# First modulation weights in four pairs, two token-feature tiles normed and projected per pair

## What is computed

```
mod   = silu(c)     @ w_mod[0] + b_mod[0]      # 6 x 1024 values for latent tokens
mod_c = silu(c_ctx) @ w_mod[0] + b_mod[0]      # the same for context tokens
y = x * rsqrt(mean(x*x) + eps)                 # RMS norm over the 1024 features of each token
h = y * g_norm1 * (1 + scale) + shift          # shift, scale: the first two of the 6 parts of mod
z = h @ w_in                                   # combined input projection, 12 slots of 256 columns
```

## Time and profile before

| | us |
|---|---|
| median of three runs | 1928.3 |
| profiled execution | 1930.06 |
| its span, first to last instruction | 1927.5 |
| first matmul of the projection (L2343) | 50.94 |
| first matmul of slot 2 (L2533) | 85.80 |
| PE busy over the span | 1772.6 (92%) |

### The profile page before, as it was taken

One profiled execution on the slowest core, in us unless ns is written; L12 is line 12 of the kernel. 1 busy time (PEld: TensorE's weight loads), 2 busy tenths in 40 slices (PEclk: granted clock), 3 DMA queues, 4 the chain that ended last, 5 costly groups with the idle time before them and its releaser, 6 DMA issues.

```text
span 1927.5 us, 27988 instructions
## 1 busy us (share of the span) xinstructions
PE 1772.6 (92%) x11328; PEld 1533.5 (80%) x11328; DVE 1082.3 (56%) x1638; ACT 745.0 (39%) x1026; POOL 430.0 (22%) x316
## 2 busy tenths in 40 slices
PE   6898999988897999999999989999979989999998
PEld 4778897767776999989999868788667768777776
DVE  2373636676626798796987956555666342213132
ACT  3522325643214643534535463234642252323130
POOL 1231632200220000000000033452201334444542
PEclk8899999999998999999999989999898989999999
DMA  7640112100054617547266113221200212222221
GB/s 316 200 156 23 46 65 75 58 1 1 1 196 182 233 67 273 223 150 313 88 253 259 44 69 126 99 77 67 88 1 1 87 66 87 88 108 87 87 88 66
DMA packets 34432, 217.61 MB, mean 113 GB/s; under 512 B 4724, under 2 KB 5146, under 8 KB 15642
## 3 DMA queue, kind: packets, MB, share of 16 engines
q1 hardware_dynamic: 34330, 216.19, 30.7%
HBM read 196.77 MB, written 19.40 MB: 112 GB/s over the span
## 4 chain that ended last, share of the span: by engine, by line
PE 72%; DVE 12%; issue 5%; ACT 4%; DMA 3%; POOL 2%; SPq 1%; DVEq 0%; ACTq 0%; POOLq 0%
PE ps L2356 24%; PE ps L2788 20%; PE ps L2533 8%; PE ps L2343 2%; DMA raw<-w_big 2%; PE ps L2613 2%; POOL w_lo L703 2%; PE ps L2728 1%; DMA raw<-w_modl 1%; DVE xT L2085 1%; PE ps L2659 1%; DVE mx L1798 1%; PE ps L2666 1%; PE ps L2461 1%; PE ps L2297 1%
## 5 line engine op out<-in xcount | busy, mean ns | idle before, releaser
L703 POOL TENSOR_TENSOR w_lo<-raw,w_hi 128x512 fp32r<-128x512 f32 x256 | 346.5, 1384 | 1179.1 <-ACT w_hi L808 1179.1
L2788 PE MATMUL ps<-op_hi,w_hi 128*128 128x384 f32 x896 | 308.0, 344 | 21.5 <-DVE w_lo L2045 8.7
L2788 PE MATMUL ps<-op_hi,w_lo 128*128 128x384 f32 x896 | 305.1, 340 | 0.0
L2788 PE MATMUL ps<-op_lo,w_hi 128*128 128x384 f32 x896 | 305.1, 340 | 0.0
L808 ACT ACTIVATE w_hi<-raw 128x2048 fp32r<-128x2048 f32 x64 | 122.2, 1910 | 195.3 <-PE ps L2356 131.0
L2788 PEld LDWEIGHTS ps<-op_hi,w_hi 128*128 128x128 f32 x896 | 171.4, 191 | 29.1 <-issue 15.5
L2788 PEld LDWEIGHTS ps<-op_lo,w_hi 128*128 128x128 f32 x896 | 171.2, 191 | 0.0
L2788 PEld LDWEIGHTS ps<-op_hi,w_lo 128*128 128x128 f32 x896 | 171.1, 191 | 0.0
L2356 PE MATMUL ps<-h_hi,w_hi 128*128 128x512 f32 x496 | 166.7, 378 | 0.1
L2356 PE MATMUL ps<-h_lo,w_hi 128*128 128x512 f32 x496 | 161.9, 369 | 0.0
L2356 PE MATMUL ps<-h_hi,w_lo 128*128 128x512 f32 x496 | 161.8, 368 | 0.0
(11 more groups left out here) (333 smaller groups left out, 3538.2 us busy)
## 6 DMA issues: line engine op xcount, KB each, us to landing
raw<-w_big SPq DMA_DIRECT2D x96, 1024.0 KB, 4.8
raw_m<-w_modl SPq DMA_DIRECT2D x20, 1024.0 KB, 6.3
raw<-w_modl SPq DMA_DIRECT2D x16, 1024.0 KB, 5.0
op_hi<-op_cache SPq DMA_DIRECT2D x21, 768.0 KB, 4.7
op_lo<-op_cache SPq DMA_DIRECT2D x21, 768.0 KB, 6.3
first_mod<-w_modl SPq DMA_DIRECT2D x8, 1024.0 KB, 19.0
xT<-x_keep SPq DMA_DIRECT2D x2, 3072.0 KB, 10.0
op_cache<-op_hi SPq DMA_DIRECT2D x7, 768.0 KB, 3.3
```

The costliest lines, as they stand in the source:

```text
L703: ins = nc.gpsimd.tensor_tensor(w_lo[r][:, ks, :], raw[raw_r][:, ks, :], w_hi[r][:, ks, :].bitcast(F32), ALU.subtract)
L2788: ins = mm(bank(base + g, 0, h), wide(w)[:, k, g * P:(g + 1) * P], ops[hl][:, k, 0:h], start=(p in FRESH and k == 0 and q == 0), stop=(k = ...
```

## The change

Six edits, all in the opening of layer 0:

1. SP loads projection weight 0 first, then the modulation tiles in the order 0, 4, 1, 5, 2, 6, 3, 7, so that shift and scale of two feature tiles come together; then projection weight 1, tile 8 and the masks.
2. ACT squares each token tile out of PSUM beside its copy; DVE sums each over its 8 feature tiles with one reduction (`tile_sum`), in place of squares and additions by feature tile.
3. Rows, columns, bias and gain are made pair by pair (`first_rows`, `first_columns`, `first_gain`). Pairs 0 and 1 go ahead of the projection. The row products of pairs 2 and 3 stand inside `feature_pair` before k = 2 and k = 4, their columns before k = 3 and k = 5. DVE copies the rows of pair j between mult 2(j-1) and mult 2(j-1)+1, and makes the gain of pair j before mult 2j.
4. The low part of projection weight 0 is made by DVE in one piece, not by POOL.
5. ACT splits projection weight 1 after tile k = 5, not after k = 7; DVE makes the masks after the norm.
6. The row product of tile 8 moves into `feature_pair`, before k = 6; that of tile 9 moves out of it, to group (0,1).

```diff
-    first_at = [RS + j * SLOT for j in range(3)] + [RU + (3 + j) * SLOT for j in range(3)] + [RH, RH + SLOT]
+    first_at = [RS, RS + 2 * SLOT, RU + 3 * SLOT, RU + 5 * SLOT, RS + SLOT, RH + 2 * SLOT, RU + 4 * SLOT, w_lo_at + SLOT]
     first_mod = [place(f"first_mod{j}", a, [KD, WC]) for j, a in enumerate(first_at)]
-    mod_rows = place("mod_rows", RV + 5 * T * 4, [FIRST_MODS * WC])
-    cload = place("cload", RH + 2 * SLOT, [C_ALL - C_KEEP])
...
+    cload = place("cload", RU, [C_ALL - C_KEEP])
+    vin = place("vin", RH, [P])
+    vin1 = place("vin1", RH + P * 4, [P])
+    mod_rows = place("mod_rows", RV + 6 * T * 4, [4 * WC])
+    sqx = [place(f"sqx{j}", RV + j * D_MODEL * 4, [KD, P]) for j in range(2)]
...
-            for j in range(FIRST_MODS):
-                sp.dma_start(first_mod[j][:], mslot(j)).then_inc(slot_landed(j), 16)
+            load_w(wslot(0), 0)
+            for i in range(FIRST_MODS // 2):
+                for j in (i, FIRST_MODS // 2 + i):
+                    sp.dma_start(first_mod[j][:], mslot(j)).then_inc(slot_landed(j), 16)
+            load_w(wslot(1), 1)
+            load_mod(mslot(FIRST_MODS))
+            sp.wait_ge(sem("x_trans"), 2)
             sp.dma_start(cload[:], consts[:, C_KEEP:C_ALL]).then_inc(sem("masks_landed"), 16)
-            load_w(wslot(0), 0)
-            load_mod(mslot(FIRST_MODS))
-            load_w(wslot(1), 1)
             sp.wait_ge(sem("cs_ready"), 1)
...
-                lows(l * PROJ, l * PROJ + 2)
+                if l == 0:
+                    low(2, 1)
+                else:
+                    lows(l * PROJ, l * PROJ + 2)
...
+                if j >= 2:
+                    act.wait_ge(sem("acc_added"), j - 1)
+                nc.scalar.activation(sqx[j % 2][:], pair(j).rearrange("p (k t) -> p k t", k=KD),
+                                     ACT.Square).then_inc(sem("sq_ready"), 1)
                 nc.scalar.activation(xT[:, :, cols(j)], pair(j).rearrange("p (k t) -> p k t", k=KD),
                                      ACT.Copy).then_inc(sem("x_in"), 1)
...
-                if l == 0 and which == 1:
-                    split_hi(1)
+                    if l == 0 and which == 1 and k == 5:
+                        split_hi(1)
...
-                    for k in range(KD):
-                        square(k, T, 0)
-                norm(l, 1, T, x_total, split=0 if l == 0 else None)
+                    T_("acc").add(TILES)
+                    split_hi(0)
+                norm(l, 1, T, x_total)
...
+            def tile_sum(j):
+
+                dve.wait_ge(sem("sq_ready"), j + 1)
+                v.tensor_reduce(tmp[4][:, cols(j)], sqx[j % 2][:].rearrange("p k t -> p t k"), AX_X,
+                                ALU.add).then_inc(sem("acc_added"), 1)
+
+            def low_w0():
+
+                dve.wait_ge(sem("hi_ready"), 1)
+                v.tensor_tensor(w_lo[0][:], raw[0][:], w_hi[0][:].bitcast(F32), ALU.subtract).then_inc(sem("lo_ready"), 1)
...
-                if l == 0 and which == 1:
-                    for r in range(2):
-                        dve.wait_ge(sem("mod_used"), FIRST_MODS // 2 * (r + 1))
-                        v.tensor_copy(mod_rows[:, r * 1024:(r + 1) * 1024],
-                                      ps[:, r * 1024:(r + 1) * 1024]).then_inc(sem("mod_rows_ready"), 1)
-                    dve.wait_ge(sem("mod_cols"), 1)
-                    v.tensor_tensor(modt[0][:, 0:4 * FIRST_MODS].rearrange("p (m c) -> p m c", c=2),
-                                    bank(6, 0, 4 * FIRST_MODS).rearrange("p (m c) -> p m c", c=2),
-                                    bc(lvec(0, LV_BMOD, 2 * FIRST_MODS), 2), ALU.add).then_inc(sem("mod_out"), 1)
-
-                dve.wait_ge(sem("mod_out"), mod_n.at(1))
-                nc_ = 2 if which == 1 else 1
-                step(v.scalar_tensor_tensor(gs[:, :, 0:nc_], mt[:, m0:m0 + KD, 0:nc_], 1.0,
-                                            bc(lvec(l, LV_G1 if which == 1 else LV_G2, KD), nc_), ALU.add, ALU.mult))
+                first = l == 0 and which == 1
+
+                def first_rows(j):
+
+                    dve.wait_ge(sem("mod_used"), 2 * j + 2)
+                    v.tensor_copy(mod_rows[:, j % 2 * 512:j % 2 * 512 + 512], bank(7)).then_inc(sem("mod_rows_ready"), 1)
+
+                def first_gain(j):
+
+                    dve.wait_ge(sem("mod_cols"), j + 1)
+                    for m in (2 * j, FIRST_MODS + 2 * j):
+                        ins = v.tensor_tensor(mt[:, m:m + 2, :], bank(6, 2 * m, 4).rearrange("p (m c) -> p m c", c=2),
+                                              bc(lvec(0, LV_BMOD + m, 2), 2), ALU.add)
+                    step(ins)
+                    ins = v.scalar_tensor_tensor(gs[:, 2 * j:2 * j + 2, :], mt[:, m0 + 2 * j:m0 + 2 * j + 2, :], 1.0,
+                                                 bc(lvec(0, LV_G1 + 2 * j, 2), 2), ALU.add, ALU.mult)
+                    if j == KD // 2 - 1:
+                        ins.then_inc(sem("mod_out"), 1)
+                        dve.wait_ge(sem("mod_out"), 1)
+                    else:
+                        step(ins)
+
+                if first:
+                    first_rows(0)
+                    low_w0()
+                    first_gain(0)
+                else:
+                    dve.wait_ge(sem("mod_out"), mod_n.at(1))
+                    nc_ = 2 if which == 1 else 1
+                    step(v.scalar_tensor_tensor(gs[:, :, 0:nc_], mt[:, m0:m0 + KD, 0:nc_], 1.0,
+                                                bc(lvec(l, LV_G1 if which == 1 else LV_G2, KD), nc_), ALU.add, ALU.mult))
                 dve.wait_ge(sem("rstd_ready"), T_("rstd").add(2 if l == 1 and which == 1 else 1))
...
                 for k in range(KD):
+                    ahead = first and k > 0 and k % 2 == 0
+                    if ahead:
+                        low(k - 1)
+                        first_gain(k // 2)
                     if k >= 2:
                         dve.wait_ge(sem("h_full"), T_("hf").n + k - 1)
                     v.tensor_tensor(tmp[k % 2][:, 0:n_t], xT[:, k, 0:n_t], tmp[3][:, 0:n_t],
                                     ALU.mult).then_inc(sem("t_ready"), 1)
-                    if k == 0 and l == 0 and which == 1:
-                        make_masks()
-                    if k >= 1:
+                    if first and k % 2 == 0 and k < KD - 2:
+                        first_rows(k // 2 + 1)
+                    if k >= 1 and not ahead:
                         low(k - 1)
                 low(KD - 1)
+                if first:
+                    make_masks()
...
-            def first_mods(a, b):
-
-                for j in range(a, b):
-                    pe.wait_ge(slot_landed(j), 16)
-                    mod_rows_of(j * WC, first_mod[j]).then_inc(sem("mod_used"), 1)
-
-            def first_mods_columns():
-                pe.wait_ge(sem("mod_rows_ready"), 2)
-                for m in range(2 * FIRST_MODS):
-                    ins = mm(bank(6, 2 * m, 2), mod_rows[:, m * P:(m + 1) * P], row2, start=True, stop=True)
+            def first_rows(j):
+
+                for x in range(2):
+                    at = j + x * FIRST_MODS // 2
+                    pe.wait_ge(slot_landed(at), 16)
+                    mod_rows_of(7 * 512 + x * WC, first_mod[at]).then_inc(sem("mod_used"), 1)
+
+            def first_columns(j):
+
+                pe.wait_ge(sem("mod_rows_ready"), j + 1)
+                for x in range(2):
+                    for m in range(2):
+                        at = 2 * (j + x * FIRST_MODS // 2) + m
+                        ins = mm(bank(6, 2 * at, 2), mod_rows[:, (4 * (j % 2) + 2 * x + m) * P:(4 * (j % 2) + 2 * x + m + 1) * P],
+                                 row2, start=True, stop=True)
                 ins.then_inc(sem("mod_cols"), 1)
...
-            def feature_pair(g, r, mov, n_ts, ready, second_mod=False):
+            def feature_pair(g, r, mov, n_ts, ready, with_mods=False):
 
                 for k in range(KD):
-                    if second_mod and k == KD // 2:
-                        pe.wait_ge(sem("mod_landed"), mods.at(2) * 16)
-                        mod_rows_of(7 * 512, raw[1]).then_inc(sem("mod_summed"), 1)
+                    if with_mods and k in (2, 4):
+                        first_rows(k // 2 + 1)
+                    elif with_mods and k in (3, 5):
+                        first_columns(k // 2 + 1)
+                    elif with_mods and k == 6:
+                        mod_rows_sum()
                     pe.wait_ge(ready[0], ready[1] + k + 1)
...
-                        if has_mod and (s, m) != (0, 1):
+                        if has_mod and (s, m) != (0, 0):
                             mod_rows_sum()
...
-                    first_mods(0, 4)
-                    norm_sum(T)
-                    first_mods(4, FIRST_MODS)
-                    first_mods_columns()
+                    first_rows(0)
+                    first_columns(0)
```

(38 more changed lines are left out.)

## The result

The changed kernel took 1934.99 us (median of 13 runs, 1931.6 to 1937.5), the kernel before, run beside it, 1923.37 us (13 runs, 1922.2 to 1931.7). The ratio is 1.0045, with a 95% interval of 1.0036 to 1.0054: **8.7 us slower** (6.9 to 10.4), where 7.7 us were forecast. The ratio is not the quotient of the two medians, which lie 11.6 us apart: the runs of the kernel before fall in two groups, seven at 1922.2 to 1923.4 us and six at 1926.8 to 1931.7, and their median lies in the lower one. The 1936 of the prediction was 7.7 us on the 1928.3 of the first three runs; that it lies 1 us from the 1934.99 measured is in part luck, since the base was 5 us lower in the comparison. All ratios take the fast runs alone: one execution of experiment 1 took 2894 us at a granted clock of 0.55 and is left out.

The account below looks back on a forecast made before the run. PE, busy for 92% of the span, was taken as the bound, with loads bounding part of the opening. -14.4 + 10.5 + 5.7 + 2.0 + 3.9 = +7.7 us on 1928.3 gave 1936 us, range 1926 to 1942.

Parts of the forecast that it names:

- Step 1: Opening: weight 0 first and paired tile loads start the projection near 36.5 us, 14.4 us earlier.
- Step 2: Loop of pairs: PE and DVE wait for each other in turn, 31.0 us instead of 20.5, +10.5 us.
- Step 3: Loop of pairs: thin work and waits lower PE's clock before k = 0, 2 and 4; three falls, +5.7 us.
- Step 4: End of the loop: POOL's pieces of weight 1 and DVE's last operations exclude each other, +2.0 us.
- Step 5: From k = 7 to slot 2: tile 10's load waits for tile 9's product on one buffer, +3.9 us.
- Nothing later takes it back: After slot 2: its delay stays to the end, since PE is the bound and its stages follow each other.
- Gain kept: Rival, loop of pairs: clock holds and POOL's pieces fall between DVE's operations; 1924 to 1927 us, chance 0.12.
- Only the load wait: Rival, clock up to slot 2: it falls once, not three times; +3.9 us, 1932 us, chance 0.17.
- Not serial: Rival, loop of pairs: rows of pairs 2 and 3 are made earlier than read; -8 us, 1920 us, chance 0.05.
- Low clock for long: Rival, loop of pairs: columns and thin rows keep the clock at 0.50 for k = 2 to 5; 1940 us, chance 0.16.

Follow-up runs that it names:

- experiment 1: Changed kernel, but modulation tile 9 has a buffer of its own and is loaded in the opening; ratio 1.0007 to the kernel before.
- experiment 6: Changed kernel, but SP loads the first modulation tiles in the order 0 to 7, still behind projection weight 0; ratio 1.0090 to the kernel before.
- Experiment 3: Changed kernel, but row products and columns of pairs 2 and 3 stand two tiles earlier in PE's program; ratio 0.9969 to the kernel before.
- experiment 5: Changed kernel with matmuls of no use in PE's three waits on h_lo in the loop of pairs; ratio 1.0045 to the kernel before.
- experiment 2: Changed kernel, but ACT splits projection weight 1 after tile k = 7, as before; ratio 1.0029 to the kernel before.
- experiment 8: The kernel before, profiled again with no edit; one run, 1924.27 us, span 1921.4.
- experiment 9: Changed kernel with matmuls of no use in PE's loop waits and 15 more at group (1,0); ratio 1.0035 to the kernel before.
- experiment 4: Changed kernel with rows and columns two tiles earlier and tile 9 in its own buffer; ratio 0.9942 to the kernel before.

## Why the prediction was right

- **Step 1, head start.** Forecast 36.5 us. Five traces with that opening and a fall in it gave 36.06 to 37.59. The first profile, at full clock, gave 33.32, 3.2 us earlier: 2.2 were priced, and the row products began at 21.90, behind ACT's last copy, not at 22.7. The load order makes 6.0 to 7.6 us of the head start (experiment 6). The tile sums took 1.94 us each (11.21 for six, overlapping), 1.6 times the contiguous 1.19 of the earlier trace rows and not double. The Trainium skill (SBUF — State Buffer, on "cachelines") says that such strides cost but not how much, and these rows agree; the stride alone is not shown as the cause, since the two reductions also differ in their outputs (128 and 16). The sums ended at 22.97 and cost nothing: DVE was then idle 0.9 us until PE had made the rows of pair 0.
- **Step 2, the serial loop.** Forecast two waits of 2.75 us; measured 2.55 twice. Experiment 3 removed them by order alone.
- **Step 3, the clock.** Forecast three falls of 1.9 us, at k = 0, 2 and 4. There were three, at k = 0, 2 and 6. That the number came out was luck: k = 4 kept its clock, 1.8 us less than forecast, and k = 6 and 7 lost theirs for some 5.7 us and took 7.0 us, not 4.2, 2.8 more. The wait before k = 6, which POOL lengthened, was the longest, but why k = 4 was spared is not shown. The loop as a whole, steps 2 to 4, was forecast at 38.7 us and took 39.1 in both traces. The falls are shown (experiment 5: 35.0 us without those at k = 2 and 6); what they cost in total time is not.
- **Step 4, POOL beside DVE.** Forecast 2.0, measured 2.6 us at k = 6 (4.13 less 1.53): from the columns of pair 3 to k = 6 it took 4.9 us in experiment 2, where 4.8 were forecast, and 7.5 with POOL beside. Gain, mults and the low of k = 6 were stretched; the last low, after POOL's pieces, took 0.96. The rule of the Trainium skill (SBUF — State Buffer, on the exclusive lock of the shared port pair) held for the mults and lows, of which no row of before told.
- **Step 5, two row products in a row.** Forecast 19.9 us from k = 7 to slot 2; measured 20.2 and 20.1. Removing the wait gave 7 us (experiment 1). The weak term is the credit of 1.7 us, for a slot 2 that would keep its clock where the old one lost it. It held beside the first profile of before; in the second the old slot 2 kept its clock too (experiment 8), and from k = 7 to slot 2 took 12.5 us, not 14.3. That could be why it is 8.7 and not 7.7 us; two profiles do not show how often it falls. The forecast of slot 2 "near 93.5" took this credit off too early: its own steps give 36.5 + 38.7 + 19.9 = 95.1. Measured were 92.61 and 96.64.
- **Nothing later takes it back.** The prediction said so, and for the change itself it held within the noise (slot 2 late by 6.8 and 10.8 us, the total by 8.7 and 10.6). It does not hold for the clock: beside the second profile of the changed kernel, experiment 5 reached slot 2 6.6 us earlier and experiment 9 8.3, but by the ratios they gained 1.9 and 3.9 us, and experiment 5 none beside the first ratio.
- **The rivals.** *Gain kept* needed k = 7 to end by 67.7; it ended at 72.4 and 76.5. *Only the load wait* had one fall; there were three. *Not serial* is refuted by the two waits. *Low clock for long* did not happen for k = 2 to 5.

## What to carry to other kernels

An early start is worth only what the loop behind it can take: when two engines hand work to each other inside it, put every producer at least one turn ahead of its consumer, and look for a blocking wait of DVE with useful work queued behind it. When a use moves later past another use of the same buffer, the next load moves with it, and a hidden 5 us becomes a wait. Putting the row products and columns two tiles earlier made a loss of 0.45% a gain of 0.3%, and a second buffer made it 0.6%.

## What the runs showed of the hardware that was not expected

- One kernel's opening came out at either clock: 33.32 or 37.41 us to the first projection matmul, in two executions of the same program. A single profile can be 4 us off in the first 40 us.
- The same thin work did not always bring a fall: in the changed kernel the clock fell before k = 2 and not before k = 4, both after row products of 1.93 us and a wait of 2.55, and at group (1,0) it fell in experiment 4 and not in experiment 1.
- Two executions of the kernel before reach slot 2 at 85.80 and 85.78 us, with falls at different places on the way, and end 6.1 us apart.
- A reduction that steps over 128 fp32 elements took 1.94 us for 1024 elements a row (128 outputs), where a contiguous one takes 1.19 (16 outputs).
